# Two mixers and two feed-forward blocks on one core: spare banks for two product tiles, a later order for the q and k norms, and a layout of the scratchpad on multiples of 2,048 bytes

## The reference, cut to what matters

```python
def first_block(x, ...):
    nx = rmsnorm(h, attn_norm_g[l])
    proj = jnp.einsum('bsd,dp->bsp', nx, w_in[l])          # 1024 -> 3088
    o_a = gla_mixer(gq, gk, gv, glog)                      # 4 heads, normed, gated
    o_b = dilated_mixer(dq, dk_, dv_, rel_bias)            # 8 heads, 3 branches
    h = h + jnp.einsum('bsm,md->bsd', mixed, w_out[l])
    a = jnp.square(jax.nn.relu(jnp.einsum('bsd,df->bsf', nm, w_ff1[l])))   # 4096
    h = h + jnp.einsum('bsf,fd->bsd', a, w_ff2[l])
    return rmsnorm(h, final_norm_g)

def hybrid_layer(x, ...):
    proj = rms_norm(x, norm1_g) @ w_in                     # 1024 -> 5632
    q = rms_norm(heads(q_sb), q_norm_g)                    # per head of 64 channels
    k = rms_norm(heads(k_sb), k_norm_g)
    o_sb = stick_breaking_attention(q, k, heads(v_sb))
    o_hg = hgrn2_mixer(q_hg, f_hg, i_hg, g_hg, lb, hg_norm_g)
    mixed = jax.nn.sigmoid(gate_sb) * y_sb + jax.nn.sigmoid(gate_hg) * y_hg
    h = x + mixed @ w_out
    ffn = (jax.nn.silu(hn @ w_gate) * (hn @ w_up)) @ w_down   # 2816 hidden
    return h + ffn
```

## Time and profile before

| | us |
|---|---|
| median of three runs | 1453.48 |
| lowest and highest | 1453.12, 1454.0 |
| the profiled execution's own time | 1452.93 |
| its span, first to last instruction | 1451.6 |
| PE busy in the span | 1411.3 (97%) |
| ACT busy | 864.7 (60%) |
| DVE busy | 621.0 (43%) |
| POOL busy | 203.4 (14%) |

### The profile page before, as it was taken

How to read it: one execution, slowest core, us unless ns; L and a number is a source line. 1 busy time by engine, 2 the same in 40 slices (tenths; PEclk the granted TensorE clock), 3 DMA queues, 4 the chain that set the end, 5 groups by cost and what they waited for, 6 DMA issues and landing times.

```text
span 1451.6 us, 17691 instructions
## 1 busy us (share of the span) xinstructions
PE 1411.3 (97%) x6886; PEld 1132.8 (78%) x6886; DVE 621.0 (43%) x1177; ACT 864.7 (60%) x1267; POOL 203.4 (14%) x230
## 2 busy tenths in 40 slices
PE   6999999999999999998999999999999999999999
PEld 4877866788888888866867778887788888888887
DVE  4043466521211212355378779864534321331232
ACT  5475566653644535664578778767566654673562
POOL 3111100111111111110100100001111111111110
PEclk9999999999999999999999999999999999999999
DMA  6776643698888888875755556659888888888875
GB/s 213 184 180 147 156 105 83 162 202 190 192 185 197 192 183 199 185 164 118 156 120 120 130 123 146 160 145 242 232 197 190 194 193 183 200 192 185 193 169 123
DMA packets 72935, 247.93 MB, mean 171 GB/s; under 512 B 8242, under 2 KB 8258, under 8 KB 72724
## 3 DMA queue, kind: packets, MB, share of 16 engines
q0 software_dynamic: 31536, 113.54, 45.9%
q1 hardware_dynamic: 40452, 131.67, 27.1%
q10 hardware_dynamic: 864, 1.60, 0.3%
HBM read 240.45 MB, written 6.32 MB: 170 GB/s over the span
## 4 chain that ended last, share of the span: by engine, by line
PE 79%; ACT 8%; DVE 8%; issue 3%; DMA 2%; POOL 0%; DVEq 0%; ACTq 0%; POOLq 0%
PE bank L404 24%; PE bank L406 24%; PE bank L408 23%; ACT WH L696 2%; PE bank L582 2%; PE bank L514 1%; ACT WL L704 1%; DVE eb L1322 1%; DMA RAW<-in_w_out 1%; ACT eb L850 1%; PE bank L533 1%; PE bank L557 1%; DMA RAW<-in_w_in 1%; PE bank L547 1%; PE bank L565 1%
## 5 line engine op out<-in xcount | busy, mean ns | idle before, releaser
L404 PE MATMUL bank<-NH,WH 128*128 128x512 f32 x1152 | 471.3, 409 | 12.7 <-ACT NH L677 7.0
L406 PE MATMUL bank<-NL,WH 128*128 128x512 f32 x1152 | 453.0, 393 | 1.5 <-DVE NL L1068 1.0
L408 PE MATMUL bank<-NH,WL 128*128 128x512 f32 x1152 | 452.2, 393 | 0.1
L696 ACT ACTIVATE WH<-RAW 128x1024 fp32r<-128x1024 f32 (+2 forms) x227 | 235.3, 1037 | 223.6 <-PE bank L408 209.2
L404 PEld LDWEIGHTS bank<-NH,WH 128*128 128x128 f32 x1152 | 218.4, 190 | 80.9 <-issue 32.5
L406 PEld LDWEIGHTS bank<-NL,WH 128*128 128x128 f32 x1152 | 218.6, 190 | 49.9 <-issue 4.3
L408 PEld LDWEIGHTS bank<-NH,WL 128*128 128x128 f32 x1152 | 218.1, 189 | 47.0 <-POOL WL L1652 0.6
L704 ACT ACTIVATE WL<-WH 128x1024 fp32r<-128x1024 f32 (+2 forms) x219 | 229.6, 1048 | 5.6
L406 PE MATMUL bank<-AL,WH 128*128 128x512 f32 x432 | 170.7, 395 | 0.0
L408 PE MATMUL bank<-AH,WL 128*128 128x512 f32 x432 | 170.6, 395 | 0.0
L404 PE MATMUL bank<-AH,WH 128*128 128x512 f32 x432 | 170.6, 395 | 0.0
(11 more groups left out here) (276 smaller groups left out, 1653.3 us busy)
## 6 DMA issues: line engine op xcount, KB each, us to landing
RAW<-in_w_in SPq DMA_DIRECT2D x64, 512.0 KB, 4.9
RAW<-in_w_ff SPq DMA_DIRECT2D x64, 512.0 KB, 6.0
WL<-in_w_ff POOLq DMA_DIRECT2D x64, 512.0 KB, 8.6
WL<-in_w_in POOLq DMA_DIRECT2D x62, 512.0 KB, 7.7
RAW<-in_w_gu SPq DMA_DIRECT2D x44, 512.0 KB, 6.3
WL<-in_w_gu POOLq DMA_DIRECT2D x44, 512.0 KB, 8.7
RAW<-in_w_down SPq DMA_DIRECT2D x20, 512.0 KB, 4.8
WL<-in_w_down POOLq DMA_DIRECT2D x20, 512.0 KB, 8.5
```

Source lines behind the costliest of these rows:

```text
L404: e.matmul(o, a[0], a[1], start=(k == 0), stop=False)
L406: e.matmul(o, b[0], b[1], start=False, stop=False)
L408: mm = e.matmul(o, c[0], c[1], start=False, stop=(k == t.kt - 1))
L696: e.activation(WH[p % HL][:, 0:n], RAW[p % RAWS][:, 0:n], ACT.Copy).then_inc(*act.sig("high", p))
```

## The change

The change has three parts.

1. Tile kG 1 (the fourth product tile of all) and tile qS 3 (the fourth of the second mixer) go to the bank OB instead of one of GB's three. They wait for OB's last reader alone, and the other tiles take turns without them, so each tile waits for the one three before it in that turn.
2. The steps of the q and k norms behind the evacuation get planned times of their own, `qk_time`: at least 12.4 apart from the tile two before and 2 from the last, the square at +0.2, the mean at +7.5, the root at +7.7 and DVE's part from +8.7. The time at which the second mixer's scale is planned moves from `T_DS + 6.3` to `T_DS + 15.0`.
3. The layout: `small` and part of the masks stand at the bottom, WH begins at byte 18,432, and with that WH, WL, RAW, hT, NH, NL, cf, rs, acc, sq all begin at multiples of 2,048. `mark` is 133,120, also a multiple, so AH1, AL1, AH2, AL2, mh and ml are too (AH1 at 133,120, mh at 157,696, ml at 194,560). `resets` and `gains` go to the top; the masks are cast in two instructions on POOL instead of one.

```diff
@@ Plan
+SPARE = {("kG", 1), ("qS", 3)}
...
+        turn = []
...
                 t = Tile(len(self.tiles), u, c, len(mine), st, kt, cols, sets, v, v + kt * (0.5 if nat else 1.0))
+                t.spare = (st, len(mine)) in SPARE
+                t.bank, t.last = len(turn) % 3, turn[-3] if len(turn) >= 3 else None
+                if not t.spare:
+                    turn.append(t)
@@ build_program, the layout
+        sm = sb("small", 184)
+        marks = sb("marks", 9 * P, U8)
+        lev_mask = [marks[:, i * P:(i + 1) * P] for i in range(7)]
+        diag_mask = marks[:, 7 * P:8 * P]
+        gla_mask = marks[:, 8 * P:9 * P]
+        top[0] = (top[0] + PAGE - 1) // PAGE * PAGE
         WH = [sb(f"WH{i}", PIECE, F32R) for i in range(HL)]
...
-        cu = sb("cu", 9 * P + 3 * S, U8)
...
+        rs, acc = sb("rs", S), sb("acc", S)
+        sq = two("sq")
+        mark = top[0]
+        assert mark % PAGE == 0
+        top[0] = mark + 46 * PAGE
+        resets = sb("resets", 3 * S, U8)
+        reset = [resets[:, i * S:(i + 1) * S] for i in range(3)]
...
-        sm = sb("small", 184)
-        rs, acc = sb("rs", S), sb("acc", S)
-        sq = two("sq")
-        mark = top[0]
-        cu_at = nc.sbuf_usable_end // 64 * 64 - (9 * P + 3 * S) * 4
+        top[0] = mark
+        cu_at = mark + 46 * PAGE - (9 * P + 3 * S) * 4
...
+        assert all(x % PAGE == 0 for x in (sb_end_at, hq_at))
@@ banks
+        def bank_for(t):
+            return OB if t.spare else GB[t.bank]
...
-                    bank = GB[t.g % 3]
+                    bank = bank_for(t)
...
-                        if k == 0 and t.g >= 3:
-                            pe.wait_ge(freed(plan.tiles[t.g - 3]))
+                        if k == 0 and t.spare and ob["free"]:
+                            pe.wait_ge(ob["free"])
+                        if k == 0 and not t.spare and t.last:
+                            pe.wait_ge(freed(t.last))
...
+                            if t.spare:
+                                ob["free"] = freed(t)
@@ times of the q and k norms
-        ready = {..., "n_second": T_DS + 6.3}
+        ready = {..., "n_second": T_DS + 15.0}
...
+        qk_start = []
+        for t in plan.stage["qS"] + plan.stage["kS"]:
+            qk_start.append(max(due(t), qk_start[-2] + 12.4 if len(qk_start) > 1 else 0, qk_start[-1] + 2 if qk_start else 0))
+
+        def qk_time(t, more):
+            return qk_start[t.i + (4 if t.st == "kS" else 0)] + more
...
             def qk_means(st):
                 for t in plan.stage[st]:
-                    yield due(t, 5.0)
+                    yield qk_time(t, 7.5)
...
-                    yield due(t, 1.2)
+                    yield qk_time(t, 0.2)
                     act.wait_ge(freed(t), *back)
                     e.activation(wT[u], o, ACT.Square).then_inc(*act.sig("qk_square", st, t.i))
-                    yield due(t, 5.2)
+                    yield qk_time(t, 7.7)
...
-                    yield due(t, 6.0)
+                    yield qk_time(t, 8.7)
                     root_square(key, y, a)
-                    yield due(t, 7.0)
+                    yield qk_time(t, 9.7)
                     root_better(key, bank_of(*bank), a)
                     give(bank, ("dve_root", key, 1))
-                    yield due(t, 8.0)
+                    yield qk_time(t, 10.7)
@@ gpsimd
-                e.tensor_copy(cu, cu_f).then_inc(*pool.sig("masks"))
+                e.tensor_copy(marks, cu_f[:, 0:9 * P])
+                e.tensor_copy(resets, cu_f[:, 9 * P:]).then_inc(*pool.sig("masks"))
```

More of the change, by code:

```diff
@@ L27 @@
 RAWS = 3
+PAGE = 2048
 DOWN = [(0, 8), (8, 16), (16, 22)]
@@ L211, in build_program @@
         gmask = cf[:, 4 * P:4 * P + S]
-        cu = sb("cu", 9 * P + 3 * S, U8)
-        lev_mask = [cu[:, i * P:(i + 1) * P] for i in range(7)]
-        diag_mask = cu[:, 7 * P:8 * P]
-        gla_mask = cu[:, 8 * P:9 * P]
-        reset = [cu[:, 9 * P + i * S:9 * P + (i + 1) * S] for i in range(3)]
+        rs, acc = sb("rs", S), sb("acc", S)
[5 more added lines that the diff above has]
+        reset = [resets[:, i * S:(i + 1) * S] for i in range(3)]
         gv_ = sb("gains", 8 * 5 + 4 + 2 + 2 + 1 + 8)
@@ L356, in build_program @@
         T_DS = plan.start("qS") + 8
[L357 removed]
+        ready = {"n_attn": 17.3, "n_mlp": mean_time["mlp"] + 3.3, "n_ffn": mean_time["ffn"] + 3.3, "n_second": T_DS + 15.0}
         def due(t, more=1.0):
             return max(t.v1, ready[operands[t.st][2]]) + more
+        qk_start = []
[3 more added lines that the diff above has]
+            return qk_start[t.i + (4 if t.st == "kS" else 0)] + more
         def up_time(t, more):
@@ L725, in natural @@
                     yield max(t.v1 + 1, ready_columns[ph])
-                    j, c, bank = t.i % NT, t.i // NT, GB[t.g % 3]
+                    j, c, bank = t.i % NT, t.i // NT, bank_for(t)
                     act.wait_ge(("product", "tile", t.g), ("scale_columns", ph))
@@ L1144, in put @@
                     yield due(t)
-                    bank, ph = GB[t.g % 3], scale_of[operands[t.st][2]]
+                    bank, ph = bank_for(t), scale_of[operands[t.st][2]]
                     dve.wait_ge(("product", "tile", t.g), ("scale", ph), *waits)
```

23 lines of the change are left out of this document (11 added, 12 removed).

## The result

The changed kernel takes 1421.7 us (median of 4 runs, 1419.5 to 1423.0), against 1453.3 us of the kernel before. The ratio is 0.9781, with an interval of 0.9764 to 0.9797: 31.6 us faster by the medians. Forecast: 1421.0.

A forecast was written before the change was run, and what follows sets the result against it. PE was taken as the bound, busy 1411.3 of 1451.6 us, losing time to idling, low clock and late matmul starts. 1452.9 - 9.5 - 13.2 - 9.8 = 1420.4, or 1421.0 at the median; own range 1416 to 1428, wider range 1405 to 1441.

The forecast's parts named there:

- The walk: Fourth tile and second mixer's q and k: new order stepped through with trace durations, giving 9.8 and 13.9 us less.
- The 0.3 us taken off for weights: Fifth tile: third weight piece lands at 39 to 40, PE comes at about 39.7, so 0.3 us less gain.
- all later loads wait for PE's progress and move with it: Loads behind the first four tiles: they shift with PE; no cost was put on them.
- 0.7 was taken off: Second mixer's q and k: 13.9 us gain cut to 13.2 for margins of 2 us read from one execution.
- Rival C: Second mixer's norms: a new wait replaces those at the means, half to all of 13.2 us lost, about 1430; 13 in 100.
- where it was said that one would show: Second mixer's banks: a late root holds DVE's evacuations and through a bank PE; any new wait would appear there.
- a choice among readings: Layout: rows stand to weights as NH to WH, all at 0.2267 us, -9.8 us; total 1421, 46 in 100.
- B: Layout: place doesn't help AH, which stays above byte 131,072 at 0.2333 us; 1430.8 us; 22 in 100.
- D: Layout: rows starting at a multiple lose nothing, up to 85 us gained, 1346 at the end; 11 in 100.
- a shortage of reading: Products at full clock: 13 of NH's 227 ns are no work and vanish when the engine reads more slowly.
- E: Layout: rows beginning at multiples of 256 are slow, NH's and natural products lose 27.9 us, 1458.7 us; 8 in 100.
- the two rules weighed in the prediction: Layout: independent ports make it worth nothing, 1430.8; N / 2.4 + 2.5 ns would make it 64 us or more.

The follow-up runs named there:

- each scan: Changed kernel with the AH and AL rows of seven stages at many distances from the weights, weights at 0 or 128; single runs, not compared in time.
- the finer one: Changed kernel with each of 56 AH and AL rows at its own distance from the weights, 0, 4, 8 to 220 bytes modulo 256; time not compared.
- the scan with the weights at 128: Changed kernel with AH and AL rows of seven stages at 54 places and weights 128 bytes past a multiple of 2,048; single run, time not compared.
- the run that keeps the spare bank: Changed kernel with the second mixer's norm times of before, its fourth q tile still on the spare bank; 1434.9 us, ratio 0.9879.

## Why the prediction was right, point by point

**Part 1.** Forecast -9.5, measured -9.4 in the stage (30.5 against 39.9), and 8.7 when undone alone (39.2). The mechanism is the forecast one, the wait and the half clock behind it. That the size fits so closely is in part luck. The rows of PE from the fourth tile's first matmul across its first band matmul (L443, now L473), and the stretch of the whole tile:

```profile
28.58 0.39 PE L432 MATMUL bank<-NH,WH 128*128 128x512 f32 x1
...
29.03 0.39 PE L436 MATMUL bank<-NH,WL 128*128 128x512 f32 x1
29.35 1.02 PE L473 MATMUL bank<-mixed,rel 33*8 33x512 f32 x2
...
30.64 0.39 PE L434 MATMUL bank<-NL,WH 128*128 128x512 f32 x1
```

```profile
28.58:37.55 8.97, 8.97 (x38) 5.42 (x36) 6.23 (x9) 3.63 (x6) 2.94 (x3) 1.00 0.84 220
```

The walk had 8.2 us for this tile, and it lasts 8.97 without a wait, so the tile is worth 9.0 and not 9.8. A band matmul takes 30.64 - 29.03 - 2 x 0.2267 = 1.16 us, where the walk took 0.86 from a matmul of 128 rows, and L435's records (now L465) take 1.18 instead of 1.05. The 0.3 us taken off for weights was spent here: L465 starts at 35.77 and the fifth tile at 37.55, neither with a wait. The remaining 0.35 us of the gain lies in the first three tiles, which the change doesn't touch and which ran that much faster in this execution (21.53 against 21.88 us; a wait of 0.5 us for NL, there before, is absent).

What did come late was one stage further:

```profile
52.11 0.39 PE L436 MATMUL bank<-WL,NH 128*128 128x256 f32 x1 [0.68 <-DMA WL<-in_w_in]
```

The walk said that "all later loads wait for PE's progress and move with it". That holds for when this load is issued. POOL issues it, before and after:

```profile
49.65 0.86 POOL L1648 DMA_DIRECT2D WL<-in_w_in  x1 [3.30 <-ACT WL L704]
```

```profile
40.25 0.86 POOL L1678 DMA_DIRECT2D WL<-in_w_in  x1 [3.03 <-ACT WL L734]
```

PE comes to the piece some 11 us later in both. But its last packet lands at 57.7 before (8.1 us) and at 51.7 after (11.4 us). The step that failed, if a small one, is therefore that the walk moved the loads and kept their durations. With the idle time gone the transfers stand closer together: the DMA share is 0.84 in the fourth tile, where it was 0.48. That this is what makes the transfer longer is likely and not tested. It cost 0.9 us. The wait isn't in every kernel: of the nine with part 1 in them whose times were compared, six show it near 52 us, at 0.4 to 1.3 us, and three don't, in which the piece lands at 50.0 to 51.1; the two without part 1, the kernel before among them, don't either.

**Part 2.** Forecast -13.2, measured -13.9 (13.3 in q and k and 0.5 in v, 13.85 before rounding): the walk's own figure before 0.7 was taken off. The walk's times can be held against the trace, less 13.6 us by which the stage begins earlier. Squares on ACT, then means on PE, of the fourth tile of q and the second of k:

```profile
648.50 0.64 ACT L927 ACTIVATE wT<-qS 128x512 f32<-128x512 f32 x1 [2.67 <-DVE qS L1439]
...
660.59 0.63 ACT L927 ACTIVATE wT<-kS 128x512 f32<-128x512 f32 x1 [2.19 <-DVE qS L1439]
```

```profile
652.18 1.02 PE L595 MATMUL bank<-wT,cf 128*128 128x512 f32 x2
...
662.80 1.02 PE L595 MATMUL bank<-wT,cf 128*128 128x512 f32 x2
```

The square of qS 3 ends at 649.1 (walk: 662.7 - 13.6 = 649.1) and is read at 652.2 (walk: 652.1). That of kS 1 ends at 661.2 (walk: 660.9) and is read at 662.8 (662.6): the smallest margin of all is 1.6 us, forecast 1.7. Rival C needed this margin to fail. It didn't, and no wait came at a bank either, where it was said that one would show. The last evacuation of k runs from 670.8 to 671.5, forecast 671.3.

**Part 3.** Forecast -9.8 for 1,488 products of 6.6 ns, measured -8.4 in AH's stages and -1.0 in mh's. About half of the shortfall is in mh: the walk took AH's 233.3 ns for it, and its products stood at 232.4 in the kernel before. The reason was right as well: the relative place of rows and weights. It was a choice among readings that two samples fitted equally well, given 46 in 100, and that it was the right one was luck as far as the trace of before goes; the experiments decided it. The unit was not seen. The text spoke of multiples of 2,048, and the runs show multiples of 256. Moving rows and weights together changes nothing (all at 1,792: 1422.2), moving the weights alone does (at 128: 1444.5).

B is out, since AH still lies above byte 131,072 and runs at 226.7. D is out for the places tried: in each scan, the finer one included, no place away from a distance of 0 has a mean below the 226.7 that rows at 0 take. Its evidence, no loss at the lower clock, was true. The prediction called the 13 ns that remain a shortage of reading; no run shows what they are, and no layout tried here wins them. E is out on both sides: its slow rows (1,792) are fast once the weights stand there too, and the weights alone make NH slow.

This also bears on the two rules weighed in the prediction. Moving the weight buffers by 128 bytes costs 23.5 us with the same rows. The Trainium skill, "SBUF — State Buffer", section "Who interferes with whom", gives PE independent ports for the moving operand and the weight load; by that rule no move of a buffer changes PE's pace. The traces here disagree: in this kernel products of 512 columns start 2 to 8 ns later (distances at multiples of 32) unless row and weights lie a multiple of 256 bytes apart. Whether it is the two ports that meet, the traces don't tell.

At half clock the distance is 427 ns for 512 columns (six starts from 661.79 to 664.35 in the kernel before), and at full clock no stage's mean was below 226.7, 13.2 ns over half of 427. The Trainium skill, "TensorE: Matmul & The Clock Gate", section "Wait — 56ns, not 53.3ns?", puts that extra at about 2.5 ns for bf16; the lower clock agrees with its N / 1.2, the extra doesn't carry over to these float32r products.

**The sum.** -9.5 - 13.2 - 9.8 = -32.5 was forecast for the profiled execution, -31.7 came. The errors are +0.1 (part 1: 0.5 on the tile, less 0.35 in the three ahead of it), +0.9 (the load behind it), -0.7 (margins not needed) and +0.4 (part 3). They partly cancel, so the 0.7 us between forecast and median is closer than the single terms are.

## What to carry to other kernels

Read the distance from start to start of undisturbed matmuls for each operand apart; if two operands of one shape differ, look at how they lie to the weight buffers, and try to place all of them at one rest modulo 256 bytes. When a wait on the bound engine goes, follow the loads for two stages behind it, and don't take their durations as fixed. A spare bank is worth nothing while something ahead of it in the engine's order waits for the same evacuation or a later one: walk the new order with durations from the trace, and keep the walk's times, since they can be checked one by one.

## What the runs showed of the hardware

- The pace of products of 512 columns of float32r depends on the distance between moving row and weights modulo 256 bytes: 226.7 ns at 0, 229 at 64, 232 to 234 at the other multiples of 32. Natural products of 256 columns (WH moving, a slice of NH loaded) showed no loss when the weights were moved by 128 bytes: they start every 119.6 ns at a distance of 0, 118.6 with both weight buffers at 128 and 117.3 with WL alone there. So the rule of the long products isn't theirs.
- Off the distance of 0 the starts aren't even. At 128 AH's alternate in the kernel before (229 and 237 to 238 ns in turn). mh's there begin so too, but behind a short stop they go through seven unlike ones (228 to 241 ns), 232.4 in the mean, and so do AH's in the scan with the weights at 128. A pair of neighbours reads like a fault of the trace; only the mean over many starts gives the pace. Why one distance has two patterns these runs don't show.
- With only WL out of step, the start of the WL product and the one after it are late, by 5.8 and 7.4 ns; the third isn't.
- A float32 matmul of two records with 512 columns takes PE 0.87 us from start to start with 128 rows and 128 columns of weights (means, 638.8 to 662.8) and 1.16 with 33 rows and 8 columns (L473): the small one costs more.
- Idle stretches of much the same length were followed by half clock at different moments or not at all. Behind 3.39 us it covered the mean in the earlier trace rows (records of 2.08 us) and began 1.05 us behind the mean's start in the run that keeps the spare bank (records of 1.12 us). Behind 3.59 us in the changed kernel it lasted 3.4 us; behind 3.30 us in the run with the attention earlier products start 0.23 us apart, and none came. What decides it these runs don't show.
